# A trunk of macaron blocks on one core: the first norm weights on another queue, weight quarters first, one clock-keeping product less

## The reference

```
def rms_norm(x, g):
    y = x * rsqrt(mean(x * x, -1) + 1e-6)
    return y * g

def swiglu_ffn(h, w_up, w_down):
    gate, up = split(h @ w_up, 2)
    return (silu(gate) * up) @ w_down

for l in range(2):
    x = x + 0.5 * swiglu_ffn(rms_norm(x, norm_ffn1[l]), ffn1_up[l], ffn1_down[l])
    ...                       # pooling mixer and latent attention, gated, added to x
    x = x + 0.5 * swiglu_ffn(rms_norm(x, norm_ffn2[l]), ffn2_up[l], ffn2_down[l])
return rms_norm(x, final_norm)
```

## Time and profile before

| | us |
|---|---|
| median of 3 runs | 1090.31 (1090.27 to 1090.43) |
| the profiled execution, its own time | 1091.61 |
| its span, first to last instruction | 1089.8 |
| TensorE products busy | 1081.5 |
| VectorE busy | 888.5 |
| ScalarE busy | 650.6 |
| from the span's start to the first real weight product | 6.75 |

### The profile page before, as it was taken

How to read it: one execution, slowest core, us unless ns; L and a number is a source line. 1 busy time by engine, 2 the same in 40 slices (tenths; PEclk the granted TensorE clock), 3 DMA queues, 4 the chain that set the end, 5 groups by cost and what they waited for, 6 DMA issues and landing times.

```text
span 1089.8 us, 15433 instructions
## 1 busy us (share of the span) xinstructions
PE 1081.5 (99%) x5309; PEld 907.1 (83%) x5309; DVE 888.5 (82%) x1163; ACT 650.6 (60%) x828; POOL 80.1 (7%) x102
## 2 busy tenths in 40 slices
PE   9999999999999999999999999999999999999997
PEld 6888888988988888888888888888899888888886
DVE  5989988766887698988889988986678777988895
ACT  5656655656953565665565655746469446565563
POOL 0034410200200000000000000001012000000001
PEclk9999999999999999999999999999999999999999
DMA  8576585753455555655646567748444554656651
GB/s 274 192 226 216 174 302 181 248 168 121 166 171 177 175 192 194 195 190 192 210 146 224 173 206 261 240 124 277 140 143 156 193 178 151 223 167 199 220 172 60
DMA packets 140235, 207.44 MB, mean 190 GB/s; under 512 B 5224, under 2 KB 103728, under 8 KB 139680
## 3 DMA queue, kind: packets, MB, share of 16 engines
q1 hardware_dynamic: 137472, 196.89, 55.2%
q0 software_dynamic: 2144, 9.12, 2.4%
q10 hardware_dynamic: 576, 0.85, 0.2%
HBM read 205.66 MB, written 1.05 MB: 190 GB/s over the span
## 4 chain that ended last, share of the span: by engine, by line
PE 99%; DVE 0%; issue 0%; POOL 0%; POOLq 0%; ACT 0%; DVEq 0%
PE psum L1676 31%; PE psum L1678 31%; PE psum L1677 31%; PE psum L1766 2%; PE psum L1694 2%; PE psum L1758 1%; PE psum L1954 1%; PE psum L1968 0%; PE psum L2103 0%; PE psum L2001 0%; PE psum L2003 0%; POOL xs L658 0%; DVE xs L1248 0%; DVE x L1066 0%; DVE small_T L1199 0%
## 5 line engine op out<-in xcount | busy, mean ns | idle before, releaser
L1072 DVE TENSOR_TENSOR w_lo<-raw,w_hi 128x1024 fp32r<-128x1024 f32 (+6 forms) x279 | 412.2, 1503 | 75.6 <-ACT w_hi L686 74.8
L1676 PE MATMUL psum<-w_hi,xT 128*128 128x512 f32 (+2 forms) x984 | 382.9, 389 | 0.0
L1678 PE MATMUL psum<-w_hi,xT 128*128 128x512 f32 (+2 forms) x984 | 379.3, 385 | 0.0
L1677 PE MATMUL psum<-w_lo,xT 128*128 128x512 f32 (+2 forms) x984 | 378.7, 385 | 0.0
L686 ACT ACTIVATE w_hi<-raw 128x2048 fp32r<-128x2048 f32 (+5 forms) x167 | 284.5, 1709 | 71.7 <-PE psum L1678 66.4
L1676 PEld LDWEIGHTS psum<-w_hi,xT 128*128 128x128 f32 x984 | 184.7, 188 | 39.1 <-DVE w_lo L1072 1.0
L1678 PEld LDWEIGHTS psum<-w_hi,xT 128*128 128x128 f32 x984 | 184.7, 188 | 37.1
L1677 PEld LDWEIGHTS psum<-w_lo,xT 128*128 128x128 f32 x984 | 184.9, 188 | 34.6 <-issue 0.2
L803 ACT ACTIVATE oT<-xs 128x1024 fp32r<-128x1024 f32 x72 | 76.5, 1062 | 69.9 <-DVE xs L1072 69.9
L771 ACT ACTIVATE scores<-psum,stat 128x256 f32<-128x256 f32 x88 | 41.2, 473 | 111.6 <-PE psum L1678 110.8
L1072 DVE TENSOR_TENSOR oT<-xs,oT 128x1024 fp32r<-128x1024 f32 x72 | 88.0, 1229 | 0.0
(11 more groups left out here) (214 smaller groups left out, 1416.0 us busy)
## 6 DMA issues: line engine op xcount, KB each, us to landing
raw<-ffn_up_dram SPq DMA_DIRECT2D x170, 512.0 KB, 4.9
raw<-ffn_down_dram SPq DMA_DIRECT2D x44, 1024.0 KB, 4.8
raw<-w_in_dram SPq DMA_DIRECT2D x20, 1024.0 KB, 5.3
raw<-w_attn_proj_dram SPq DMA_DIRECT2D x8, 1024.0 KB, 5.0
raw<-w_out_dram SPq DMA_DIRECT2D x8, 1024.0 KB, 5.2
raw<-w_uq_dram SPq DMA_DIRECT2D x8, 576.0 KB, 4.0
gates<-b_gate_dram POOLq DMA_DIRECT2D x4, 1024.0 KB, 7.4
raw<-w_ukv_dram SPq DMA_DIRECT2D x8, 512.0 KB, 3.9
```

Of the source, the lines that this page charges most:

```text
L1072: return dve.tensor_tensor(dst, a, b, ALU.subtract)
L1676: nc.tensor.matmul(dst, a_hi, b_hi, start=first, stop=False)
L1677: nc.tensor.matmul(dst, a_hi, b_lo, start=False, stop=False)
L1678: return nc.tensor.matmul(dst, a_lo, b_hi, start=False, stop=last)
```

## The change

Three edits at the start of the program, and none elsewhere. The load of the row of norm weights moves from the head of SyncE's queue to ScalarE's, between the identity and the second x block. TensorE turns the first x tile before it turns the row of norm weights, and waits for the row only there. `KEEP` goes from 3 to 2.

```
-WARM, KEEP = 5, 3
+WARM, KEEP = 5, 2
...
-            sp.dma_start(first_gain, gains[0:1, :].rearrange("o (k n) -> (o k) n", k=KD)).then_inc(gain_row_landed, 16)
             for L in range(DEPTH):
                 ffn(L, 0)
...
                 act.dma_start(x[:, t, half(0)], x_in[0, blk(t), half(0)]).then_inc(x_landed[0][t], 16)
                 if t == 0:
                     act.dma_start(ident[:, :], c_ident).then_inc(ident_landed, 16)
+                    act.dma_start(first_gain, gains[0:1, :].rearrange("o (k n) -> (o k) n", k=KD)).then_inc(gain_row_landed, 16)
...
             keep_clock(4, WARM)
             pe.wait_ge(ident_landed, 16)
+            turn_first(0, 0)
             pe.wait_ge(gain_row_landed, 16)
             nc.tensor.transpose(psum[:, 1, 0:KD], first_gain, ident[0:KD, 0:KD]).then_inc(gain_turned, 1)
-            turn_first(0, 0)
             keep_clock(5, KEEP)
```

## The result

| | kernel before | changed kernel |
|---|---|---|
| median, us | 1090.53 | 1092.07 |
| lowest to highest of the executions compared, us | 1090.18 to 1091.05 | 1091.26 to 1093.18 |
| ratio of the changed kernel to the one before | | 1.0015, 95% interval 1.0009 to 1.0021 |
| the profiled execution, us (span) | 1091.61 (1089.8) | 1092.67 (1090.9) |

The change costs 1.5 us. That is a small loss, under the 0.2% named above as the least a measurement tells, though with 22 runs of the kernel before and 21 of the changed one the interval is narrow enough to leave 1 out. One more execution of the changed kernel took 2212.22 us, twice the time of all others; it is left out, and nothing here explains it. The forecast was 1090.1, with a range that ended at 1091.2. The runs of the changed kernel also spread over 1.9 us, those of the kernel before over 0.9 us.

What follows compares the result with a forecast made beforehand. The first weight quarter's landing at 6.62 us was taken as the bound; a load 0.40 us earlier, half kept at the slow clock, took 0.20 from 1091.61 to 1091.41, less 1.3 to the median: 1090.1 us, range 1088.9 to 1091.2.

Steps and rivals of the forecast that it cites:

- The bound, the first weight quarter at 6.62: Start of TensorE's weight products: the first quarter's landing at 6.62 us ends the wait before the load at 6.72.
- The keeping products' 0.3 us: TensorE before its first weight load: the keeping products free the array at about 6.42, 0.3 us before the bound.
- SyncE's part, a quarter 0.4 us earlier: SyncE's queue without the gain row: the first weight quarter lands 0.4 of a possible 0.49 us earlier, at 6.22.
- The identity: TensorE's wait behind the warming products: the identity has landed at 4.02 us, and the turned tiles still load from there.
- the sum: Start of the weight products: first load at 6.32 in place of 6.72, half of 0.40 us kept, giving 1090.1 us.
- rival B: Start of TensorE's work: identity or gain row comes late, slower; 1090.6 for an identity 0.9 us late; chance 0.14.
- The gain row in the longer queue: ScalarE's queue behind the identity: the row lands at 4.14, at the far bound 7.04, and is wanted at about 4.72.
- The swap, "worth nothing": TensorE turns x before the gain row: worth nothing itself, VectorE begins at about 5.5, within 0.05 us of before.
- One keeping product, "covers nothing": TensorE before the first weight product: dropping one product of 0.43 us frees the array at 5.99; it covers nothing.
- The clock: TensorE's first weight products: clock rises from 1.2 to 2.4 GHz at about 10.29 us, so half of 0.40 us is kept.
- C: Rival at TensorE's start: more idling without the keeping product makes the clock rise 3.41 us later; 1091.8 us; chance 0.09.
- D: Rival at TensorE's start: the clock is up from the start of the weight products, 1.71 us won; 1088.5; chance 0.07.

Runs made afterwards that it cites:

- e8: The kernel before, unchanged, profiled a second time: median 1090.37 us, ratio 0.9999 to the kernel before.
- e1: The kernel before with two clock-keeping products in place of three, nothing else: median 1091.08 us, ratio 1.0006 to the kernel before.
- e4: The changed kernel with the load of the row of norm weights back at the head of SyncE's queue: median 1090.77 us, ratio 1.0007 to the kernel before.
- e9: The kernel before with three warming products in place of five: median 1090.82 us, ratio 1.0006 to the kernel before.
- e11: The kernel before with no clock-keeping products in place of three: median 1092.00 us, ratio 1.0010 to the kernel before.
- e14: The kernel before with no warming products in place of five: median 1091.19 us, ratio 1.0005 to the kernel before.
- e2: The changed kernel with three clock-keeping products again in place of two: median 1092.16 us, ratio 1.0017 to the kernel before.
- e3: The kernel before with only the load of the row of norm weights moved, to ScalarE's queue behind the identity: median 1091.76 us, ratio 1.0012.
- e5: The changed kernel with eight warming products in place of five: median 1090.62 us, ratio 1.0001 to the kernel before.
- e12: The changed kernel with eight warming and three clock-keeping products in place of five and two: median 1090.57 us, ratio 1.0000 to the kernel before.
- e15: The changed kernel with no warming products in place of five: median 1092.30 us, ratio 1.0015 to the kernel before.
- e6: The changed kernel with the identity issued ahead of x on ScalarE's queue: median 1093.09 us, ratio 1.0023 to the kernel before.

## Why the prediction was wrong, point by point

- **The bound, the first weight quarter at 6.62.** Right for the kernel before: in e8 the array and VectorE are free long before, since its clock was up by then, and the load still comes at 6.82. In e1, e4, e9, e11 and e14, with the quarters issued at 1.22 too, the first lands after 4.9 to 5.1 us, at 6.1 to 6.3, and the load comes at 6.22 to 6.43. (The keeping products' 0.3 us is counted to the load at 6.72; to the quarter it is 0.2.)
- **SyncE's part, a quarter 0.4 us earlier.** Right in direction and far too small. It landed 2 us earlier, at 4.6, in 3.8 us where 5.0 to 5.5 were expected. The reading of the earlier trace rows that the engines had room from 3.5 us on was right; what it left out is that the room in front of it, at 2.5 to 3 us, was where the identity passed. None of the 2 us was won, because the load then waited for VectorE.
- **The identity.** This is the first step that failed, twice over. The prediction read 4.02 as the identity's landing, though its own rows 4 and 5 give 3.65 and the warming products held the array until then. And the sum kept 4.02 and left the identity's delay to rival B. It landed 1.1 us later, which moved the load to 4.79, and to 4.79 to 5.11 in all six profiles in which the quarters were issued at 0.73 and it stood behind x (the changed kernel, e2, e3, e5, e12, e15). The Trainium skill ("DMA: Bandwidth & Descriptors", "Issuing engines are not separate DMA queues"), which the prediction names beside the words "with the identity and x paying for it", says that the transfers interleave, and the shares above agree: ScalarE's packets fell from 157 to 47 in the half microsecond that counts.
- **The gain row in the longer queue.** Not a cost: TensorE's load of it stands at 5.83 with 0.33 us ahead of it, for which the profile names no wait, in the changed kernel.
- **The swap, "worth nothing".** Right as far as e4 can tell. VectorE begins 1.57 us after the first turned tile's load, where 1.5 was expected.
- **One keeping product, "covers nothing".** Wrong. It covered for the clock. Without it ten of the 22 executions of e1 and e4 lose more than a microsecond. In the changed kernel its lack no longer matters (e2).
- **The clock.** The second step that failed, and the larger. The sum took the rise at 10.29 from one execution as a fixed instant, halved what was won before it, and carried "1.3 us above the median" over as a constant. But by e8 the 1.3 us was for the most part the effect itself: that execution's clock rose late, and those timed mostly rose before the first weight product, by their times. The question was not by how much work moves against a fixed rise but whether the change moves the rise. The changed kernel pays 2.2 us from the first weight load on by its profile, where e8 pays nothing.
- **The rivals.** B had the path: an identity 0.9 us late with a load at 7.2 (measured: 7.10). It priced this at 1090.6, because it too held the rise fixed. C had the clock, at 9 in 100, and its 1091.8 is near the measured 1092.07 by luck. It asked for a rise 3.41 us after 10.29 and more than five slow passes, and the profile shows a rise at 11.6 behind four slow passes and slow turned tiles, as many passes as the forecast had; and C gave its price against the median, whose executions, if they are like e8's, have no slow passes to begin with. Of its two reasons the longer idle time fits e5 and e12, and the missing product doesn't (e2). D's 1088.5 comes to 1088.6 by its own terms, or 1088.4 with the 0.20 of the forecast.
- **What the page says of the clock.** The Trainium skill ("TensorE: Matmul & The Clock Gate", Part 1, "What's actually happening") says that the gate's observation runs freely and isn't reset when the kernel starts; I took that for a fixed instant in the program, while the page draws the opposite from it, that the instant differs between executions. The runs agree with the page that it differs, and by far more than the half microsecond to either side that the page gives: the rise was at 10.4 and at 5.6 in two profiles of the same kernel.

## What to carry to other kernels

In the first microseconds of this kernel the small transfer that everybody waits for must not share its time with bulk that nobody can use yet: a 4 KB load at the head of the bulk queue was a useful delay. Look for that before moving a transfer to the front. Fill TensorE's waits up to the moment its real work starts, and count warming products by whether they leave a gap, not by how many there are; whether they do is seen in the products' rows and not in the loads'. A wait that the profile names is no proof either: issue time plus transfer time tells whether the thing had long been there. And before a profile's clock is built into a sum, see whether its time is that of the median execution; one that lies 1.3 us above executions that agree within 0.16 us is telling something.

## What was unexpected of the hardware

- The first weight quarter, 256 KB, took 4.9 to 5.5 us to land when issued at 1.22 (the kernel before twice, e1, e4, e9, e11, e14), and 3.8 to 4.2 us when issued at 0.73 beside x and the identity in the same order on the other queue (the changed kernel, e2, e3, e5, e12, e15).
- The clock's rise lies anywhere from 4.7 us (e4's profile) to 12.2 us (e6's), and at 10.4 and 5.6 for the same program.
- Five warming products ahead of a stretch of 1.43 us without a load (0.7 us without a product) are worth 0.2 us by the medians, inside the noise; three more that close it 1.45 us.
